# 8 KB weight rows in seven slots, a rearranged first expert pair, and the last pair added by TensorE, in a one-core decoder step

## What is computed

```python
g_top, g_idx = lax.top_k(softmax(xt @ w_group_router + b), 1)          # 4 groups
e_top, e_idx = lax.top_k(softmax(logits_of_that_group), 2)             # 2 of 8 experts
weights = g_top * (e_top / jnp.sum(e_top, axis=-1, keepdims=True))
for gi in range(N_GROUPS):                                             # 32 experts, D=1024, D_EXPERT=256
    hg = jax.nn.silu(xt @ w_gate[e]) * (xt @ w_up[e])
    y = y + (hg * combine[:, e]) @ w_down[e]
h = h + y
return rmsnorm(h, norm_final)
```

## Time and profile before

| | us |
|---|---|
| median of 3 runs | 879.12 |
| the profiled execution's own time | 877.38 |
| its span, first to last instruction | 875.4 |
| PE busy | 786.9 |
| DVE busy | 290.4 |
| ACT busy | 258.4 |
| POOL busy | 80.5 |

### The profile page before, as it was taken

The page is one execution under the profiler, slowest core; times in us unless marked ns, Lnnn a source line. Parts: engine busy times, 40 slices in busy tenths (PEclk is TensorE's granted clock), DMA queues, the critical chain, the costliest instruction groups (busy, mean ns, idle before and its releaser), DMA issues.

```text
span 875.4 us, 12710 instructions
## 1 busy us (share of the span) xinstructions
PE 786.9 (90%) x5304; PEld 632.2 (72%) x5304; DVE 290.4 (33%) x516; ACT 258.4 (30%) x463; POOL 80.5 (9%) x122
## 2 busy tenths in 40 slices
PE   4999999999999999999999999998999978788730
PEld 4999999999989899999999999974333323232210
DVE  6223255664273542112465543151000000000017
ACT  6225544444311232413222120403232222112102
POOL 2000001000203010000000000310111111000004
PEclk9999999999999999999999999988999999889975
DMA  9512131113336341232124378485899999999835
GB/s 236 152 49 85 61 96 49 49 49 97 121 104 218 111 146 53 91 98 82 63 87 168 97 286 324 158 291 223 306 410 411 409 409 408 407 406 404 349 137 215
DMA packets 83335, 173.22 MB, mean 198 GB/s; under 512 B 13266, under 2 KB 50642, under 8 KB 82708
## 3 DMA queue, kind: packets, MB, share of 16 engines
q1 hardware_dynamic: 76292, 154.28, 48.5%
q0 software_dynamic: 6992, 18.21, 5.8%
HBM read 161.96 MB, written 17.90 MB: 205 GB/s over the span
## 4 chain that ended last, share of the span: by engine, by line
PE 73%; SPq 15%; DMA 4%; DVE 4%; ACT 2%; issue 2%; POOL 1%; POOLq 0%; ACTq 0%; DVEq 0%
PE ps L1590 51%; SPq L399 12%; PE ps L1929 6%; PE ps L1946 3%; SPq L404 3%; DMA wgu<-w_up 2%; PE ps L1700 1%; PE ps L1848 1%; PE ps L1759 1%; PE ps L1921 1%; PE ps L1606 1%; PE ps L1608 1%; PE ps L1748 1%; PE ps L1712 1%; PE ps L1714 1%
## 5 line engine op out<-in xcount | busy, mean ns | idle before, releaser
L1590 PE MATMUL ps<-xh,wh 128*128 128x288 f32 x832 | 185.2, 298 | 0.2 <-DVE wl L1053 0.2
L1590 PE MATMUL ps<-xh,wl 128*128 128x288 f32 x832 | 182.8, 295 | 0.0
L1590 PE MATMUL ps<-xl,wh 128*128 128x288 f32 x832 | 182.6, 295 | 0.0
L1929 PE MATMUL ps<-wgu,gx 128*64 128x512 f32 x512 | 125.0, 638 | 22.3 <-DMA wgu<-w_up 21.9
L1053 DVE TENSOR_TENSOR wl<-raw,wh 128x2048 fp32r<-128x2048 f32 x36 | 83.0, 2305 | 174.2 <-ACT wh L721 174.1
L1590 PEld LDWEIGHTS ps<-xh,wh 128*128 128x128 f32 x832 | 135.3, 188 | 4.0 <-issue 3.0
L1590 PEld LDWEIGHTS ps<-xh,wl 128*128 128x128 f32 x832 | 135.4, 188 | 0.0
L1590 PEld LDWEIGHTS ps<-xl,wh 128*128 128x128 f32 x832 | 135.3, 188 | 0.0
L1929 PEld LDWEIGHTS ps<-wgu,gx 128*64 128x64 f32 x512 | 41.2, 146 | 103.8 <-issue 103.0
L721 ACT CAST wh<-raw 128x2048 fp32r<-128x2048 f32 x36 | 68.6, 1906 | 53.5 <-PE ps L1590 30.8
L1532 DVE SCALAR_TENSOR_TENSOR hm<-ps,xg,si 128x256 f32<-128x256 f32 x16 | 7.7, 484 | 220.7 <-ACT si L985 220.7
(11 more groups left out here) (312 smaller groups left out, 975.5 us busy)
## 6 DMA issues: line engine op xcount, KB each, us to landing
wgu<-w_gate SPq DMA_DIRECT2D x64, 512.0 KB, 11.2
wgu<-w_up SPq DMA_DIRECT2D x64, 512.0 KB, 17.0
wd<-w_down SPq DMA_DIRECT2D x32, 1024.0 KB, 18.7
raw<-w_in SPq DMA_DIRECT2D x26, 1024.0 KB, 5.3
raw<-w_gla_out SPq DMA_DIRECT2D x4, 1024.0 KB, 5.2
raw<-w_o SPq DMA_DIRECT2D x4, 1024.0 KB, 5.2
y<-moe_results SPq DMA_DIRECT2D x4, 1024.0 KB, 8.0
moe_rows<-h POOLq DMA_DIRECT2D x4, 520.0 KB, 3.0
```

The source lines that it names most:

```text
L1590: last.append(mm(out, left(a, k), right(b, k, o), start=k == 0 and n == 0, stop=k == k_tiles - 1 and n == 2))
L1929: ins = mm(ps[half * B:(half + 1) * B, bank, :].rearrange("t (n c) -> t n c", n=2), x[:, k, half * B:(half + 1) * B], w[half][:, :, :].rea ...
```

## The change

Four things are changed, all behind the mixer.

1. **Weights.** A partition of a slot holds 8 KB of neighbouring rows (`RB = 8`, for down `(p k)`), and is loaded by one transfer of 1 MB. Transposes take their columns with the new stride. There are seven slots; expert 6 is loaded once all rows of `h` are in DRAM, since its slot lies over `h`. Refills follow `gu_full`, but experts 7, 8, 30 and 31 (`HALVED`) still come in halves.
2. **First pair.** ACT copies the last two transposed tiles before it squares the last one. SiLU's table is loaded early by an activation whose result nobody reads. The table of extra blocks goes ahead of gate and up of pair 0; SiLU of pair 0 ahead of `gx` of pair 1; the transposes of pair 2 behind down of pair 0. `keep_awake` is called with 5 (8 before), 4 (4), 18 (11), and its call ahead of gate and up of pair 0 is gone.
3. **Last pair.** Its result isn't scattered. Zeros are, from `xg[2]`, ahead of that buffer's first gather. ACT copies the result with a weight per row, and PE adds it to each tile of tokens with a one-hot matrix (`hot_l`) in PSUM.
4. **End.** `h` is read back from DRAM into `hf`. Second results of tiles 2 to 4 are added by PE with a diagonal matrix of weights (`diag`), the others by DVE; DVE then adds PSUM to `hf`.

```diff
-SLOTS = 6
+SLOTS = 7
-RB = 4
+HALVED = (SLOTS, SLOTS + 1, NE - 2, NE - 1)
+RB = 8
...
-            return w[0, e].rearrange("(a p b) c -> p a (b c)", p=P, b=RB)
+            return w[0, e].rearrange("(p b) c -> p (b c)", b=RB)
...
+            load_gate_up(sp, 5)
             load_down(sp, 5)
+            sp.wait_ge(rows_out, 16 * NT)
+            load_gate_up(sp, 6)
+            load_down(sp, 6)
+            for i in range((NE - SLOTS + 1) // 2):
+                refill = [e for e in (2 * i + SLOTS, 2 * i + SLOTS + 1) if e < NE]
+                sp.wait_ge(gu_half, i + 1)
...
+                sp.wait_ge(gu_full, i + 1)
...
+                        load_gate_up(sp, e)
+                sp.wait_ge(dn_full, i + 1)
+                for e in refill:
                     load_down(sp, e)
...
+            for i in range(3):
+                load_rows(i)
...
-            for i in range(GX):
+            for i in range(GX - 1):
                 gather(i)
-            for i in range(NP):
+            pool.indirect_dma_start(
+                out=res_d, out_offset=bass.IndirectOffsetOnAxis(ap=slotd[:, NP - 1:NP].bitcast(U32), axis=0),
+                in_=xg[GX - 1][:, 0:D], in_offset=None, bounds_check=2 * T - 1, oob_is_err=False).then_inc(z_out, 16)
...
+            pool.wait_ge(z_out, 16)
+            gather(GX - 1)
+            for i in range(NP - 1):
...
             block_t(0)
+            silu(0)
             block_t(1)
-            silu(0)
-            for i in range(NP):
+            result(0)
+            block_t(2)
+            silu(1)
...
-                step_(stt(hv, y2[i][0:n, 0, :], wts[0:n, 0, i:i + 1], hv, ALU.mult, ALU.add))
-                stt(hv, y2[i][0:n, 1, :], wts[0:n, 1, i:i + 1], hv, ALU.mult, ALU.add).then_inc(hf_ready, 1)
+                c(stt(hv, y2[i][0:n, 0, :], wts[0:n, 0, i:i + 1], hv, ALU.mult, ALU.add))
+                if i < 2:
+                    c.sync()
+                    c(stt(hv, y2[i][0:n, 1, :], wts[0:n, 1, i:i + 1], hv, ALU.mult, ALU.add))
...
+                tt(hv, hv, ps[0:n, b:b + 2, :], ALU.add).then_inc(hf_ready, 1)
...
-            keep_awake(4)
-            experts_gate_up(0)
             pe.wait_ge(hotx_ready, 1)
             mm(ps[0:1, UB + 1, P:2 * P], xfc[:, :], ident[:, :], start=True, stop=True)
-            table(UB + 1, hot_x, XP).then_inc(tabx_full, 1)
+            table(UB + 1, hot_x, XP, hot_r).then_inc(tabx_full, 1)
+            experts_gate_up(0)
...
+            table(UB + 1, hot_w, 1, col=2 * P).then_inc(tabx_full, 1)
             experts_t(1)
...
+                for o in range(2):
+                    ins = mm(ps[0:n, b + o, :], hot_l[t][:, 0:n], yb[(NP - 1) % 2][:, o * 512:(o + 1) * 512],
+                             start=True, stop=t < 2)
+                if t >= 2:
+                    pe.wait_ge(y2_in[t], 32)
+                    for o in range(2):
+                        ins = mm(ps[0:n, b + o, :], diag[t - 2][0:n, 0:n], y2[t][0:n, 1, o * 512:(o + 1) * 512],
+                                 start=False, stop=True)
```

More of the change, by code:

```diff
@@ L298, in build @@
         junk = sb("junk", [P, D], at=zone_h + 4 * NT * DX)
-        y2 = [sb(f"y2{i}", [P, 2, D], at=None if i else zone_a) for i in range(NT)]
+        hot_r = sb("hot_r", [P, 2, NT, B], at=zone_h + 4 * NT * DX)
+        hot_w = sb("hot_w", [P, 2, NT, 2])
+        hf = sb("hf", [P, NT, D], at=slot_at[4])
+        nlb = sb("nlb", [P, D])
+        assert place[0] <= slot_at[4] + SLOT
+        y2 = [sb(f"y2{i}", [P, 2, D], at=None if i else slot_at[5]) for i in range(NT)]
         yo = [sb(f"yo{i}", [P, D]) for i in range(2)]
-        assert place[0] <= zone_b
+        assert place[0] <= slot_at[6] + SLOT
         ps = ctx.enter_context(nc.psum_tensor("ps", [P, 8, 512], F32))
@@ L509, in _, with load_rows @@
             load_down(sp, 3)
-            for a in range(2):
-                load_gate_up(sp, 5, a)
+            load_gate_up(sp, 5)
             load_down(sp, 5)
[L513 to L521, removed]
-                    load_down(sp, e)
[L523 to L526, removed]
+            sp.wait_ge(rows_out, 16 * NT)
[5 more added lines that the diff above has]
+                for e in refill:
+                    if e in HALVED:
+                        load_half(sp, e, 0)
+                sp.wait_ge(gu_full, i + 1)
+                for e in refill:
+                    if e in HALVED:
+                        load_half(sp, e, 1)
+                    else:
+                        load_gate_up(sp, e)
+                sp.wait_ge(dn_full, i + 1)
+                for e in refill:
+                    load_down(sp, e)
+            def load_rows(i):
+                n = ND if i == NPT else P
+                sp.dma_start(hf[0:n, i, :], rows_d[i * P:i * P + n, 0:D]).then_inc(y2_in[i], 16)
+            for i in range(3):
+                load_rows(i)
             nx = sp.value_load(xinfo[0:1, XB:XB + 1], min_val=0, max_val=XP)
-            sp.wait_ge(dn_full, NP)
             with sp.If(nx > 0):
+                sp.wait_ge(dn_full, NP)
                 with sp.Fori(0, XP) as j:
@@ L951, in _ @@
             square_h(0)
-            for i in range(NT - 1):
+            for i in range(NT - 2):
                 square_h(i + 1)
                 copy_ht(i)
+            copy_ht(NT - 2)
             copy_ht(NT - 1)
+            square_h(NT - 1)
             act.wait_ge(w_exp, 1)
@@ L960, in _ @@
             act.activation(rt["ex"][:], rt["dd"][:], ACT.Exp).then_inc(r_act, 1)
+            act.activation(gnh[:, 2:3], gnh[:, 0:1], ACT.Silu)
             def scaled_block(dst, ready):
@@ L994, in result @@
                     act.wait_ge(y_out[i % 2], 16 * (i // 2))
-                copy(yb[i % 2][:, :].rearrange("p (a c) -> p a c", a=2), ps[:, 2:4, :]).then_inc(yb_ready, 1)
+                if i == NP - 1:
+                    act.wait_ge(ws_ready, 1)
+                act.activation(yb[i % 2][:, :].rearrange("p (a c) -> p a c", a=2), ps[:, 2:4, :], ACT.Copy,
+                               scale=wslot[:, 0:1] if i == NP - 1 else 1.0).then_inc(yb_ready, 1)
             block_t(0)
+            silu(0)
             block_t(1)
-            silu(0)
-            for i in range(NP):
+            result(0)
+            block_t(2)
+            silu(1)
+            for i in range(1, NP):
                 if i + 2 < NP:
@@ L1515, in _ @@
             step_(tt(wts[:, 1, :], wts[:, 0, :], r["ex"][:, :], ALU.mult))
+            for k in range(2):
+                ins = tt(hot_w[:, k, :, :], hot_e[:, k, :, NE - 2:NE], wide(wts[:, k, :], 2), ALU.mult)
+                if k:
+                    ins.then_inc(hotx_ready, 1)
+                else:
+                    c(ins)
             def extra_table():
```

194 lines of the change are left out of this document (137 added, 57 removed).

## The result

The changed kernel takes 866.35 us (median of 865.13, 865.8, 866.9 and 867.01) beside 879.05 us before on the same chip: a ratio of 0.9854, 95% interval 0.9841 to 0.9867. So the gain is 12.7 to 15.1 us, where 21.5 were forecast. The two intervals of one kernel hardly touch, so kernels less than about 2.5 us apart are not told apart by medians here, and the traces are used for such steps.

What follows compares the result with a forecast made beforehand. Behind the mixer, weight loads on the DMA engines bound the kernel, then a serial tail; L 17.4 us earlier plus tail 4.0 less gave 21.4 us, span 854.0, median 857.5 us, range 848 to 868.

Steps and rivals of the forecast that it cites:

- L: Moment PE begins to multiply the weight stream's last half: 831.45 us before, forecast 814.0, 17.4 us earlier.
- Ahead of pair 0: Before the first gather: copying before squaring and fewer keep_awake calls save 2.2 us; slots table ends at 582.5.
- First gather: Gather for pair 0 meets expert 6's load: takes 9 us instead of 4.5, landing at 592.5 against 590.3.
- Pair 0: From the first gather's landing on: gate and up from 596.0 to 603.1, pair 1 at 612.4 instead of 615.9.
- The stream: Weight loads up to L: 71.3 MB at 427 GB/s take 167.0 us, plus 26.7 for gathers, scatters and uneven end.
- The tail: From L to the end of the span, with the last pair off the scatter chain: 39.9 us, 4.0 less.
- 8 KB rows are no faster: Rival for the weight stream: longer rows bring no higher rate, L comes 7.3 us later: 865 us. Chance 0.15.
- the tail gives nothing: Rival for the end: reading back and DVE bind as before: 861.5 us. Chance 0.05.
- the stream starves: Rival for refills: whole rows refill 3.6 us later, 12 refills lose 43 us in all: 900 us. Chance 0.04.
- the gather waits its whole share: Rival for the first gather: waiting behind rows twice as long, it takes 10.5 us instead of 9: 859. Chance 0.15.
- more comes back: Rival: first gather takes 7.5 us and the stream's uneven end (5.4 us) goes: 850 us. Chance 0.13.
- first gather served behind expert 6: Rival: gather lands near 596, 3.5 us late, and PE's clock falls over pair 0, some 3 more: 864. Chance 0.12.

Runs made afterwards that it cites:

- after_again: The changed kernel itself, unedited, measured a second time in another set of runs with a new profile: 863.94 us, ratio 0.9830 to the kernel before.
- late6: Changed kernel with expert 6's load held until the first gather has landed, and 13 calls of keep_awake for 18: 861.77 us, ratio 0.9786.
- rows4: Changed kernel with every weight load cut into two loads of 4 KB rows: 867.89 us, ratio 0.9871.
- early: Changed kernel with the last two tiles of rows and the norm's weights loaded right behind the first three tiles of rows: 863.86 us, ratio 0.9838.
- scatter_last: Changed kernel with the last pair scattered and read back like the others, all second results added by DVE, no one-hot or diagonal matmuls: 872.03 us, ratio 0.9925.
- early_h29: Changed kernel with the last rows and norm's weights loaded early and experts 28 and 29 loaded in halves: 865.58 us, ratio 0.9841.
- awake14: Changed kernel with nine filler matmuls of 512 columns ahead of gate and up of pair 14: 864.02 us, ratio 0.9834.
- h29: Changed kernel with experts 28 and 29 also in halves, and the first half of 30 not ahead of 29's second: 861.31 us, ratio 0.9822.
- combo1: Changed kernel with late6, early and h29 together: 859.57 us, ratio 0.9777.
- late6_rows4: Changed kernel with expert 6 held until the first gather has landed and every weight load in 4 KB rows: 864.73 us, ratio 0.9833.

## Why the prediction was right and wrong

The direction and the range were right, and the size was 8.9 us off in the median; the span came out at 864.0 and 862.2 where 854.0 was forecast. By the forecast's own moments (the last half landed at 821.8 and, in after_again, at 819.4: issue plus 20.9 us):

| stretch | forecast | changed | after_again |
|---|---|---|---|
| start to pair 1 | 612.4 | 615.6 | 613.2 |
| pair 1 to L | 201.6 | 206.2 | 206.2 |
| L to the end of the span | 39.9 | 42.2 | 42.8 |

- **Ahead of pair 0: not settled.** The seven profiles with the changed kernel's start have the table done between 581.5 and 584.6, 583.2 in the mean, against 584.7 before and 582.5 forecast. All thirteen, which share this part, lie between 581.5 and 585.1, 583.7 in the mean, and of the kernel before there is one profile. So the gain is 1.0 to 1.5 us where 2.2 were forecast, with executions 3.6 us apart.
- **First gather: right.** 9.34 and 8.70 us for 9, and 8.54 to 9.34 in the seven profiles. Alone the gather took 4.3 us (late6), beside 4 KB rows 7.81 (rows4); doubling the rows added 0.7 to 1.5, not another 3. So the 10.5 us that I had worked out by the Trainium skill's rule ("DMA: Bandwidth & Descriptors", Queues, rings and completion order) are not borne out.
- **Pair 0: about 1.5 us too long where the clock holds, 1.0 to 1.5 us too short where it does not.** SiLU's table load (1.28 us at 606.18 before) did vanish from pair 0, and pair 1 follows the slots row by 28.4 and 28.6 us without the lower clock, 31.1 to 31.6 with it; 30.1 was forecast, counted from the row's start. I had put the lower clock into a rival with a late gather, and it came with the gather on time. The mean of the seven starts of pair 1 is 613.3.
- **The stream: mis-sized, the step that failed.** "I take 427, since it is the same shape of row" read a rate off 8 us of reading back. 16 us of quiet loads gave 418 to 423 in the runs, and the stream 418 to 420. At 418.5 the 71.3 MB take 170.4 us, 3.4 more than the 167.0 of the sum. The other 1.2 us of this stretch fit the uneven end, which I had left as long as before and which is 4.4 us longer; in rows4 it is 5.2 us again (816 to 821.2), but that the 1.2 us are this is not shown. Long rows proved to be worth 4.7 us by rows4, of the 7.3 forecast. In the table above all misses have one sign: no stretch made up for another.
- **The tail: mis-sized by 2.3 to 2.9 us.** Pair 14 was complete 13.7 us before L, as forecast (13.8). It then took 8.8 to 9.7 us for 7.1; the scatter made up for it with 3.1 to 4.1 us for 6, so result rows were requested at L + 7.2 (forecast L + 8). But the rows of tile 3 landed at L + 25.6 and 26.3, not L + 22.8, and DVE stood for 4.5 and 5.3 us. From the first request to that landing the sum had 14.8 us; it took 18.4 and 19.0, and 11.4 in early, which loads `nlb` and the last two tiles of rows beforehand. So the term that was too small is what these loads cost; why they cost so much (165 GB/s from 844 to 848) is open. That last-pair work on PE stays ahead of DVE was right.
- **Rivals.** *8 KB rows are no faster* falls (rows4), *the tail gives nothing* falls (scatter_last), *the stream starves* falls (DMA share 1.02 from 660 to 800), *the gather waits its whole share* falls (8.54 to 9.34 us, not 10.5), and *more comes back* falls: the uneven end grew. The times of two rivals, 864 (*first gather served behind expert 6*) and 865 (*8 KB rows are no faster*), lie nearest, but through neither mechanism: the gather was not late, and the rows were faster. Only the lower clock over pair 0, half of the first of them, did come.

## What to carry to other kernels

Read a transfer rate from a long stretch of the same traffic, and hold it against a second stretch, before multiplying it by 70 MB: 2% of rate was 3.4 us here. A load issued early into idle engines wasn't free here, because a small transfer on the critical path started beside it; held until that transfer had landed, it was. And an end that is a chain of transfers gave little for one of its steps: what left one step earlier met the traffic ahead of it, so ask of each edit whom it will now collide with.

## What the runs showed of the hardware that was not expected

- The granted clock fell over pair 0 with a gap of 1.48 to 2.12 us in front (after_again, early_h29, awake14, the changed kernel), stayed at 1.00 with 1.51 and 1.76 (scatter_last, h29), and with none over 0.55 it fell twice (late6, combo1) and held once (late6_rows4). The length of the idle time just before does not decide it in these rows.
- Transfers beside 1 MB loads of 8 KB rows wait longer: from 580 to 700 us gathers took 8.4 to 9.1 us (medians; 7.8 and 7.3 in rows4 and late6_rows4), scatters 8.3 to 9.1 (7.2 and 7.3). A load of `w_up` took 31.3 us from issue to landing in the changed kernel (660 to 700 us), before 18.4 with half the bytes.
- The DMA engines drift apart at the end of the stream for longer with 1 MB loads of 8 KB rows (9.8 us) than with half loads of 4 KB rows (5.4 us before, 5.2 in rows4).
